# Layer 1's second feed-forward: the norm's factor at evictions in one third only, and one pair of squares summed one row block earlier

## The reference, cut to what matters

```
def _modulate(x, g, shift, scale):
    return _rmsnorm(x, g) * (1 + scale) + shift

def _swiglu(h, w1, w3, w2):
    return (jax.nn.silu(h @ w1) * (h @ w3)) @ w2

lat = lat + 0.5 * ml[8] * _swiglu(_modulate(lat, norm_ffn2_g[l], ml[6], ml[7]), *ffn2)
```

## Time and profile before

| | us |
|---|---|
| median of 3 runs | 2616.95 |
| lowest, highest | 2616.52, 2617.70 |
| the profiled execution | 2619.17 |
| its span | 2617.4 |
| PE busy | 2569.0 |
| DVE busy | 1222.5 |
| ACT busy | 1105.2 |
| POOL busy | 889.7 |

### The profile page before, as it was taken

How to read it: one execution, slowest core, us unless ns; L and a number is a source line. 1 busy time by engine, 2 the same in 40 slices (tenths; PEclk the granted TensorE clock), 3 DMA queues, 4 the chain that set the end, 5 groups by cost and what they waited for, 6 DMA issues and landing times.

```text
span 2617.4 us, 43989 instructions
## 1 busy us (share of the span) xinstructions
PE 2569.0 (98%) x17111; PEld 2290.2 (87%) x17111; DVE 1222.5 (47%) x1865; ACT 1105.2 (42%) x1538; POOL 889.7 (34%) x1092
## 2 busy tenths in 40 slices
PE   7999999999999999999999999999999999999999
PEld 5777779988897777797777798899999999999999
DVE  4222325227752232252232257675567566656754
ACT  4322333635444122244122247544674554446533
POOL 1222222320022222222222226315554455553554
PEclk9999999999999999999999999999999999999999
DMA  7443543330034334433444433234544444552454
GB/s 282 141 168 140 165 149 117 139 128 1 33 120 146 145 145 145 145 110 132 145 145 145 145 138 133 110 109 180 184 169 165 137 161 177 182 185 100 164 188 147
DMA packets 58528, 376.90 MB, mean 144 GB/s; under 512 B 6223, under 2 KB 12007, under 8 KB 14216
## 3 DMA queue, kind: packets, MB, share of 16 engines
q1 hardware_dynamic: 56988, 371.53, 39.2%
q10 hardware_dynamic: 1388, 3.16, 0.8%
HBM read 370.46 MB, written 3.16 MB: 143 GB/s over the span
## 4 chain that ended last, share of the span: by engine, by line
issue 58%; POOL 22%; PE 17%; DVE 1%; POOLq 1%; DMA 0%; ACT 0%; SPq 0%; DVEq 0%; ACTq 0%
POOL WL L1993 22%; PE PSA L583 5%; PE PSA L585 5%; PE PSA L584 5%; PE PSA L1342 0%; POOLq L405 0%; PE PSA L1240 0%; PE PSA L1267 0%; DMA X<-in_x 0%; DMA RAW<-in_weights 0%; PE PSA L665 0%; POOLq L1991 0%; ACT WH L1412 0%; PE PSA L1258 0%; PE PSA L1228 0%
## 5 line engine op out<-in xcount | busy, mean ns | idle before, releaser
L1993 POOL TENSOR_TENSOR WL<-RAW,WH 128x256 fp32r<-128x256 f32 x1088 | 889.5, 846 | 1715.3 <-ACT WH L1412 1715.3
L1412 ACT ACTIVATE WH<-RAW 128x1024 fp32r<-128x1024 f32 x544 | 545.8, 1050 | 936.6 <-PE PSA L585 918.0
L2016 DVE TENSOR_TENSOR WL<-RAW,WH 128x1024 fp32r<-128x1024 f32 x272 | 339.6, 1249 | 1077.5 <-ACT WH L1412 1077.2
L583 PE MATMUL PSA<-HH,WH 128*128 128x512 f32 (+2 forms) x1664 | 596.3, 358 | 9.4 <-DVE WL L2016 3.4
L584 PE MATMUL PSA<-HL,WH 128*128 128x512 f32 (+2 forms) x1664 | 588.6, 354 | 0.0
L585 PE MATMUL PSA<-HH,WL 128*128 128x512 f32 (+2 forms) x1664 | 588.0, 353 | 0.0
L583 PE MATMUL PSA<-GH,WH 128*128 128x256 f32 (+1 forms) x1664 | 527.0, 317 | 6.8 <-DVE GL L2033 5.7
L584 PE MATMUL PSA<-GL,WH 128*128 128x256 f32 (+1 forms) x1664 | 521.0, 313 | 0.0
L585 PE MATMUL PSA<-GH,WL 128*128 128x256 f32 (+1 forms) x1664 | 520.8, 313 | 0.0
L583 PEld LDWEIGHTS PSA<-HH,WH 128*128 128x128 f32 x1664 | 315.7, 190 | 69.0 <-issue 17.6
L585 PEld LDWEIGHTS PSA<-HH,WL 128*128 128x128 f32 x1664 | 315.8, 190 | 43.2
(11 more groups left out here) (336 smaller groups left out, 2966.1 us busy)
## 6 DMA issues: line engine op xcount, KB each, us to landing
RAW<-in_weights SPq DMA_DIRECT2D x272, 1024.0 KB, 4.8
ADA<-in_w_ada SPq DMA_DIRECT2D x65, 1024.0 KB, 4.9
Zada<-in_w_ada SPq DMA_DIRECT2D x7, 1024.0 KB, 14.5
scratch_bias<-BREL ACTq DMA_DIRECT2D x1, 2048.0 KB
SUMS<-in_c_sums SPq DMA_DIRECT2D x1, 1664.0 KB, 8.7
TB<-scratch_bias SPq DMA_DIRECT2D x1, 1536.0 KB, 11.8
X<-in_x SPq DMA_DIRECT2D x1, 1024.0 KB, 6.8
X<-in_ctx SPq DMA_DIRECT2D x1, 1024.0 KB, 9.3
```

Of the source, the lines that this page charges most:

```text
L583: pe.matmul(out, a_hi, b_hi, start=start, stop=False)
L1412: act.activation(WH[:, j, 4 * h:4 * h + 4, :], RAW[:, j, 4 * h:4 * h + 4, :], ACT.Copy)\
L1993: ins = pool.tensor_tensor(WL[:, j, kb, :], RAW[:, j, kb, :], WH[:, j, kb, :].bitcast(F32), ALU.subtract)
L2016: dve.tensor_tensor(WL[:, j, 0:4, :], RAW[:, j, 0:4, :], WH[:, j, 0:4, :].bitcast(F32), ALU.subtract)\
```

## The change

Two parts.

1. In `pair_by_stream`, `part_sums(3, 0)` moves ahead of block(0, 1, 7), the last context block of slot 0. It applies to all 4 norms by stream.
2. In layer 1's second feed-forward only third 0 keeps the 258 columns and `shifted_up`. In the down projection of third 0, DVE and ACT make the finished rows (with r and the shift) again from `X`, two channel blocks for each slot and ahead of that slot's evictions: `renewed_rows` on DVE (two scalings to `T2`, two `lower`), an ACT rounding for each block behind the slot's `split_hi`. PE waits for all 8 blocks at the start of third 1's up projection. Thirds 1 and 2 then run the plain `ffn_up` over 256 columns. The loop over the down projection's two halves is written out on ACT and DVE.

```diff
-            phase("ffn_up", ..., shifted=(l + which == 2))
+            phase("ffn_up", ..., shifted=(l + which == 2 and t == 0),
+                  renewed=(l + which == 2 and t == 1))
...
-            phase("down", 4, 4, rate, ..., first=(t == 0))
+            phase("down", 4, 4, rate, ..., first=(t == 0),
+                  renews=plan[at] if l + which == 2 and t == 0 else None)
...  # PE, weights_phase
+                if ph.get("renewed"):
+                    n.take(h_ready, KB)
...  # PE, pair_by_stream
+                        if kb == KB - 1:
+                            part_sums(3, 0)
                         block(0, 1, kb)
-                    part_sums(3, 0)
...  # ACT, down
                         after_slot(ph, it, s, 2 * ph["per"])
+                        if ph.get("renews"):
+                            for m in range(2):
+                                n.take(t_ready)
+                                kb = 4 * it + 2 * s + m
+                                act.activation(HH[:, kb, 0:N], T2[:, m, 0:N], ACT.Identity,
+                                               bias=MODS[:, ph["renews"]["mods"][0], kb, 0:1]).then_inc(hh_ready, 1)
...  # DVE
+            def renewed_rows(late, k0, N):
+                shift, scale = late["mods"]
+                for m in range(2):
+                    if k0:
+                        dve.wait_ge(h_ready, n.at(h_ready) + k0 + m - 1)
+                    dve.scalar_tensor_tensor(T2[:, m, 0:N], X[:, k0 + m, 0:N], MODS[:, scale, k0 + m, 0:1], RSTD[:, 0:N],
+                                             ALU.mult, ALU.mult).then_inc(t_ready, 1)
+                for m in range(2):
+                    n.take(hh_ready)
+                    dve.scalar_tensor_tensor(HL[:, k0 + m, 0:N], T2[:, m, 0:N], MODS[:, shift, k0 + m, 0:1],
+                                             HH[:, k0 + m, 0:N].bitcast(F32), ALU.add, ALU.subtract).then_inc(h_ready, 1)
...  # DVE, down: for each slot
                             after_slot(ph, it, per * v + s, 2 * per)
...
+                        if ph.get("renews"):
+                            renewed_rows(ph["renews"], 4 * it + 2 * v, N)
                         dve.wait_ge(mm_done, it * (2 * per) + (ph["slot"] + per * v + per))
```

More of the change, by code:

```diff
@@ L75, in ffn @@
     def ffn(l, which, rate, tokens):
+        at = len(plan)
         if l + which == 2:
@@ L85, in ffn @@
                 plan.append(dict(kind=("", "setup_loads", "setup")[t]))
-            phase("ffn_up", nb, nb, rate, tokens=tokens, blocks=nb, layer=l, third=t, shifted=(l + which == 2))
+            phase("ffn_up", nb, nb, rate, tokens=tokens, blocks=nb, layer=l, third=t, shifted=(l + which == 2 and t == 0),
+                  renewed=(l + which == 2 and t == 1))
             if l + which == 0 and t == 2:
@@ L92, in ffn @@
                 plan.append(dict(kind="decays", part=2 * t))
-            phase("down", 4, 4, rate, tokens=tokens, kin=nb, gate=2 + 6 * which, layer=l, per=1, first=(t == 0))
+            phase("down", 4, 4, rate, tokens=tokens, kin=nb, gate=2 + 6 * which, layer=l, per=1, first=(t == 0),
+                  renews=plan[at] if l + which == 2 and t == 0 else None)
     for l in range(2):
@@ L1666, in down @@
                     return body(0)
-                repeat(act, 2, body, ph is not PLAN[-1])
+                repeat(act, 2, body, ph is not PLAN[-1] and not ph.get("renews"))
                 if ph["squares"]:
@@ L2447, in down @@
                     return body(0)
-                repeat(dve, 2, body, ph is not PLAN[-1])
+                repeat(dve, 2, body, ph is not PLAN[-1] and not ph.get("renews"))
+                if ph.get("renews"):
+                    n.skip(h_ready, KB)
                 if ph["rate"]:
```

## The result

| | us |
|---|---|
| before, median of 20 runs | 2617.62 (2614.96 to 2620.82) |
| after, median of 20 runs | 2620.57 (2618.58 to 2624.78) |
| ratio, 95% interval | 1.0013 (1.0007 to 1.0019) |
| profiled execution after, its span | 2619.71, 2617.9 |

What follows compares the result with a forecast made beforehand. PE, busy 98% of the span, was taken as the bound. Terms -2.9 -1.5 -1.4 -1.4 +1.0 +6.1 +1.4 = +1.3 us on the median 2616.95 gave 2618.3, range 2615.0 to 2622.5 for 8 in 10.

Steps and rivals of the forecast that it cites:

- down 0's third slot: Third 0's down projection: evictions queued behind the remade rows make PE wait 1.0 us more; ends 0 and 1.5.
- stand ahead of up 1: Start of third 1's up projection: PE waits 6.1 us for the last remade blocks; ends 4.5 and 7.0.
- the clock behind it: After PE's stand ahead of third 1's up projection: TensorE at 1.2 GHz costs 1.4 us, or 2.8 by another row.
- two columns: Up projections of thirds 1 and 2: 256 columns instead of 258 gain 0, at the other end 0.55 us.
- down 1's wait, 2.91 to 1.4: Start of third 1's down projection: plain evictions bring GL 1.5 us earlier, cutting the 2.91 us wait; gain 1.5.
- the clock behind that wait: Behind the 2.91 us wait at down projection 1: TensorE no longer falls to 1.2 GHz; gain 1.4 us, ends 0 and 1.4.
- the weights' loop: From down projection 1's first slot: the 10.05 us RAW reload moves up with PE, keeping the gain less a few tenths.
- A: Rival, down projection 0: the four remaking instructions take 0.48 us each; sum -1.3, 2615.6; chance 0.18, with 0.05 more for faster.
- B: Rival, down projection 0: remaking stretches POOL's subtractions, deciding from 6.4 us on; +7.3, 2624.3 us; chance 0.09.
- C: Rival: 6.3 us at 1.2 GHz behind the stand, and third 1's shrunken wait still drops the clock; 2621.1; mostly 0.10.
- D: Rival: the removed waits return elsewhere (weights' loop, bank 0's Silu), losing 2 to 3 us; 2621; chance 0.06 within 0.2%.
- E: Rival: squares not ready in other norms, so 2.9 us is lost at the four places; 2621.2; chance 0.03.

Runs made afterwards that it cites:

- e1: The kernel before with only the squares' sums moved ahead of the last context block: 2614.55 us, ratio 0.9989.
- e2: The changed kernel with the squares' sums put back behind the last context block, rows still remade: 2624.50 us, ratio 1.0025.
- e5: The changed kernel with 258 columns in every matmul of up projections 1 and 2, plain evictions kept: 2621.40 us, ratio 1.0014 against the kernel before.
- e6: The changed kernel with the decays' part 2 taken ahead of up projection 1 instead of down projection 1: 2619.44 us, ratio 1.0008 against the kernel before.
- e4: The changed kernel with the remaking's factor and scaled rows in PSUM banks instead of SBUF: 2617.07 us, ratio 0.9998 against the kernel before.
- e3: The changed kernel with each pair of rows remade one slot earlier on DVE and ACT: 2612.13 us, ratio 0.9978 against the kernel before.
- e8: The changed kernel with rows remade one slot earlier, decays' part 2 ahead of up 1, factor and scaled rows in PSUM: 2608.98 us, ratio 0.9968 against before.
- e7: The changed kernel with rows remade one slot earlier and the decays' part 2 ahead of up projection 1: 2610.89 us, ratio 0.9972 against before.

## Why the prediction was right, and where it was off

| step | forecast | measured |
|---|---|---|
| part 1, four waits | -2.9 | -2.9 (e1) |
| down 0's third slot | +1.0 | +1.4 |
| stand ahead of up 1 | +6.1 | +6.3 (the wait itself 6.13) |
| the clock behind it | +1.4 | +2.5 |
| two columns | 0 | -0.1 (up to -0.6 elsewhere) |
| down 1's wait, 2.91 to 1.4 | -1.5 | -1.8 (2.91 to 1.09) |
| the clock behind that wait | -1.4 | -1.15 |
| up 2's start | 0 ("a few tenths") | +0.7 |
| down 2's wait | -1.4 | -1.6 (1.41 to 0) |
| part 2 in all | +4.2 | +6.3 |

Part 2's measured rows are changes of offset across each step, from down 0's start on, and they add up within 0.2 us.

**Right.** The mechanism and its place: the squares moved at no cost, PE's new stand behind the last low part, its size within 0.03 us, the shorter tails, no table load at the roundings, no wait in the loops of thirds 1 and 2. The instruction's length of 0.9 under POOL was read off another instruction with the same overlap, and the changed kernel's are 954 and 953 ns. At down 1 luck helped: the gain of 2.9 came out at 3.0, as the wait fell further than forecast and its clock gave back less. That the time fell inside the range, and 2 us from the forecast, rests on the range's width; the steps below were missed.

**Off: the clock behind the stand.** The prediction had two rows, 3.2 us behind a wait of 2.91 and 7 us in another stage, and took the nearer in kind. Of the four profiles with a stand of 6.13 (after, e2, e5, e6) three show 1.2 GHz for 5.4 to 5.7 us from PE's resumption on, e5 for 4.0; in all four the spell is 6.8 us long and begins within the stand. The row of 7 us would have given the size, but not as a rule: its spell stood behind a wait of only 2.81 us. This step accounts for 1.1 of the 2.1 us.

**Off: the weights' loop.** The prediction kept the 10.05 us loop, since it starts with PE, "less a few tenths", and put nothing into the sum. But in the kernel before ACT's split started 3.0 us behind PE's first matmul, at the fallen clock (1870.67, 1873.69), and DVE had ended its decays by then, 2.8 behind it. Now the split starts 1.9 behind it (1873.16, 1875.04), and the decays end 3.8 behind it, partly since a first piece of 0.15 us took 0.69 beside POOL. So they are in the way of the low part (it began at 1876.91, where A+1.10 is 1876.14) and beside POOL's four. 0.7 of the 3.0 us gained at down 1 came back here; e6 takes it away.

**Off: the third slot**, 1.4 for 1.0: evictions end at A+6.6, where A+6.5 was worked out, and PE follows 0.24 behind them, where 0.13 was taken. The rest of it stays open.

**The rivals.** A (rows at 0.48) did not happen, but e4 makes it happen, and its stand of 4.5 is then exact; the stretch in layer 1's input projection, which A put at 3.5 us, proved to be worth 2.6. B falls: POOL took 3.46, short of the 6.4 from which it decides. C was the nearest: the clock was low for 5.6 us from resumption on, where C had 6.3, though the shrunken wait dropped no clock. D happened in a small way (0.65 of its 2 to 3). E falls by e1.

## What to carry to other kernels

When rows are remade inside a running stage, what they are queued behind sets their price. Four short instructions cost 8.6 us behind the last slot's low part, which waits for PE's end, 0.9 us one slot earlier (e3), and nothing there at half their length (e8). A wait that is removed ends the time in which another engine did side work unseen; look for that work on the engine that frees the next buffer. And where DVE has two SBUF inputs beside POOL's subtractions, try one of them in PSUM: in e4 it halved the instruction.

## What the runs showed of the hardware

**TensorE's clock behind waits.** In this feed-forward waits of 0.66 to 1.41 us left it at 2.4 GHz. Behind 2.91 us it was at 1.2 GHz for 3.2 us from resumption (before; e1 has it as well). Behind 4.50 it fell 0.2 us after resumption and was back 3.6 us after it; behind 6.13 it was low for 4.0 to 5.7 (four profiles). The length of the last wait does not settle it alone. At 1669 and 1673 us of the kernel before two waits, 1.42 and 1.54 us, stand 3.5 us apart, and a spell of 6.8 us follows; all ten profiles have a spell there. A spell that begins at 607 us in the kernel before came with PE busy for all 7 us ahead of it. Rows of the kernel before:

```profile
1672.87 0.24 PE L985 MATMUL PSA<-MC,GHI 128*128 128x2 f32 x1 [1.54 <-ACT Zfm L1692]
1675.80:1682.70 6.90, 6.90 (x30) 6.51 (x31) 2.98 (x5) 1.05 (x4) 0.00 (x0) 0.51 0.00 0
600.00:607.00 7.00, 7.00 (x49) 6.37 (x47) 4.76 (x9) 5.76 (x10) 0.00 (x0) 1.00 0.00 0
```

A wait of 2.81 us in layer 1's input projection came with a fall in the kernel before, a shorter one in after and none in e3, e4, e5, e7 and e8, with the same 2.8 us. e5:

```profile
1628.19 0.39 PE L586 MATMUL PSA<-HH,WH 128*128 128x256 f32 x1 [2.81 <-POOL WL L2005]
```

```profile
1624.00:1636.00 12.00, 9.19 (x83) 8.27 (x82) 8.94 (x5) 11.72 (x11) 9.79 (x7) 1.00 0.57 203
```

PE is busy for 9.19 us in this window in both e5 and before (above), and does 83 matmuls here and 61 there. So a wait of that size may cost nothing more or, by 22 matmuls of 0.12, another 2.6 us, and two profiles can differ by that in a stage whose instructions are the same.

**DVE beside POOL.** Beside POOL's subtractions the same 128x256 instruction took 0.95 us with both inputs in SBUF and 0.48 with one of them in PSUM; with both in SBUF and POOL idle it took 0.48 as well (e3). POOL's four subtractions took 3.46 us beside the slow form and 3.00 beside the other.
